# Splitting four gate-unit weights on GpSimd behind the last token-major projection

## The reference

```
p = h @ w_in                                   # (1024 x 1024) @ (1024 x 2500)
sc, q, k, v, iq, ik, iw = split(p)
bg, cg, hv = split(sc, 3)                      # 3 x 512 columns
ya = bg * causal_dwconv(cg * hv, conv_w)       # mixer A: gated short convolution
isc = sum_h relu(iq_h . ik) * iw_h             # mixer B: indexer scores, causal
idx = top_k(isc, 256)                          # 256 keys for each query
yb = softmax(q . k[idx]) @ v[idx]              # 8 heads
x = x + concat(ya, yb) @ w_out
```

## Time and profile before

| | |
|---|---|
| median of 3 runs | 2147.96 us (2147.0 to 2148.61) |
| the profiled execution's own time | 2148.47 us |
| its span | 2146.7 us |
| TensorE busy | 2061.7 us, 96% |
| VectorE, ScalarE, GpSimd busy | 64%, 51%, 52% |
| granted TensorE clock, mean | 0.989 |

### The profile page before, as it was taken

The page is one execution under the profiler, slowest core; times in us unless marked ns, Lnnn a source line. Parts: engine busy times, 40 slices in busy tenths (PEclk is TensorE's granted clock), DMA queues, the critical chain, the costliest instruction groups (busy, mean ns, idle before and its releaser), DMA issues. The chain is left out here.

```text
span 2146.7 us, 30050 instructions
## 1 busy us (share of the span) xinstructions
PE 2061.7 (96%) x11390; PEld 1008.0 (47%) x11390; DVE 1381.4 (64%) x2019; ACT 1092.0 (51%) x1635; POOL 1116.0 (52%) x849
## 2 busy tenths in 40 slices
PE   8989977899999999999999999999999999999998
PEld 5534445644444444444444445664444444444444
DVE  7789988848674674674553045785867377467542
ACT  6468956726664664545332234542656366365520
POOL 6015442243867667657574024414386766856632
PEclk9999999999999999999999999999999999999999
DMA  4001100021112212112231011102121221211212
GB/s 179 19 11 50 35 28 2 14 64 40 51 53 65 59 47 72 55 55 59 69 106 50 0 30 35 45 12 59 40 59 45 74 59 45 74 50 50 59 45 93
DMA packets 186493, 110.20 MB, mean 51 GB/s; under 512 B 4351, under 2 KB 180902, under 8 KB 186358
## 3 DMA queue, kind: packets, MB, share of 16 engines
q1 hardware_dynamic: 185894, 107.00, 16.7%
q0 software_dynamic: 464, 1.39, 0.2%
HBM read 104.18 MB, written 4.19 MB: 50 GB/s over the span
## 5 line engine op out<-in xcount | busy, mean ns | idle before, releaser
L1318 PE MATMUL ps<-arena 128*128 128x512 f16 x2712 | 594.1, 379 | 3.9 <-DVE ps L2952 2.5
L1318 PEld LDWEIGHTS ps<-arena 128*128 128x128 f16 x2712 | 264.8, 98 | 326.6 <-DVE ps L2952 5.5
L1318 PE MATMUL ps<-h_hi,arena 128*128 128x512 f16 x1216 | 372.0, 381 | 4.7 <-DVE arena L3043 4.1
L823 POOL TENSOR_SCALAR w_scaled<-stage 128x1024 f32<-128x1024 f32 (+4 forms) x82 | 82.1, 1002 | 520.2 <-PE ps L1177 348.7
L2961 DVE SCALAR_TENSOR_TENSOR work<-ps,fvec,work 128x1023 f32<-128x1023 f32 (+1 forms) x176 | 221.6, 1279 | 22.1 <-ACT work L2107 19.0
L1318 PE MATMUL ps<-h_lo,arena 128*128 128x512 f16 x608 | 231.7, 381 | 0.0
L1318 PEld LDWEIGHTS ps<-h_hi,arena 128*128 128x128 f16 x1216 | 119.4, 98 | 151.8 <-issue 7.9
L879 POOL TENSOR_TENSOR w_scaled<-stage 128x512 f32<-128x512 f32 (+2 forms) x62 | 70.0, 1129 | 193.6 <-ACT stage L1824 193.4
L1824 ACT ACTIVATE stage<-stage 128x2048 f32<-128x2048 f32 (+2 forms) x62 | 104.5, 1686 | 112.4 <-DMA stage<-in_ffn_w_up_dram 96.1
L829 POOL TENSOR_TENSOR arena<-w_scaled,arena 128x1024 f16<-128x1024 f32 (+4 forms) x82 | 145.0, 1768 | 23.6 <-DVE srch L2723 17.6
L1177 PE MATMUL ps<-h_hi,arena 128*128 128x512 f16 x576 | 150.2, 381 | 2.1 <-ACT small L2006 1.7
(11 more groups left out here) (398 smaller groups left out, 3887.9 us busy)
## 6 DMA issues: line engine op xcount, KB each, us to landing
stage<-in_ffn_w_up_dram SPq DMA_DIRECT2D x84, 512.0 KB, 3.8
stage<-in_ffn_w_down_dram SPq DMA_DIRECT2D x48, 384.0 KB, 3.2
stage<-in_od_w_in_dram SPq DMA_DIRECT2D x20, 512.0 KB, 3.7
stage<-in_ev_w_in_dram SPq DMA_DIRECT2D x12, 512.0 KB, 3.8
arena<-in_x_dram SPq DMA_DIRECT2D x8, 512.0 KB, 5.8
stage<-in_ffn_w_down_dram SPq DMA_DIRECT2D x16, 256.0 KB, 2.7
out_dram<-arena SPq DMA_DIRECT2D x8, 512.0 KB, 3.0
stage<-in_od_w_out_dram SPq DMA_DIRECT2D x12, 256.0 KB, 2.8
```

The lines of the kernel that those rows point to most:

```text
L823: nc.gpsimd.tensor_scalar(scaled, src, W_SCALE, 1.0, ALU.mult, ALU.mult).then_inc(w_parts, 1)
L1318: last = mm(ps[:, bank, :], left, b[:, k, :], start=(fresh and k == 0 and pss == 0), stop=(k == nk - 1 and pss == 2), skip_group_check=True)
```

## The change

Gate units 2 to 5 are no longer put in the ring. GpSimd waits until all eight blocks of the token-major projection are done (`tm_done` 8) and then splits the four one behind another, into `mix_hi` rows 4 to 7 and `mix_lo` rows 0 to 3. No step of the search is waited for by these four. Units 6 and 7 take the ring's slots of units 0 and 1 and wait for these alone; units 8 to 11 wait for unit u - 2 as before. The bits at which the low parts of units 6 to 11 may start are others, and the taps and high parts of mixer A stand at other places among the splits. TensorE's order, VectorE's and ScalarE's programs and all loads are as before.

```diff
-LOW_AT_BIT = {2: 1, 3: 4, 4: 6, 5: 9, 6: 12, 7: 14, 8: 17, 9: 20, 10: 22, 11: 25}
+LOW_AT_BIT = {6: 2, 7: 6, 8: 19, 9: 22, 10: 24, 11: 26}
+AHEAD = range(2, 6)
...
+        def gate_parts(u):
+
+            if u in AHEAD:
+                return mix_hi[:, 4 + u - AHEAD[0], :], mix_lo[:, u - AHEAD[0], :]
+            return w_hi[:, u % 2, :], w_lo[:, u % 2, :]
...
+            def split_gate_unit(u, low_at=None):
+                s, (hi, lo) = u % 2, gate_parts(u)
+                ring = None if u < 6 else ring0["ev_sc"] + (u if u >= 8 else u - 4)
+                split(unit0["ev_sc"] + u, s, stage[:, s, :], w_scaled[:], hi, lo, ring, low_at=low_at)
...
-            for u in range(12):
-                split_ring(unit0["ev_sc"] + u, u, 1024, ring0["ev_sc"] + u if u >= 2 else None, LOW_AT_BIT.get(u))
-                if u >= 3 and u % 3 == 0:
-                    mixer_tap(u // 3 - 1)
-                if u >= 3 and u % 3 == 1:
-                    mixer_high(u // 3 - 1)
+            split_gate_unit(0)
+            split_gate_unit(1)
+            pool.wait_ge(tm_done, NB)
+            for u in AHEAD:
+                split_gate_unit(u)
+            split_gate_unit(6, LOW_AT_BIT[6])
+            mixer_tap(0)
+            split_gate_unit(7, LOW_AT_BIT[7])
+            mixer_high(0)
+            mixer_tap(1)
+            mixer_high(1)
+            split_gate_unit(8, LOW_AT_BIT[8])
+            mixer_tap(2)
+            split_gate_unit(9, LOW_AT_BIT[9])
+            split_gate_unit(10, LOW_AT_BIT[10])
+            mixer_high(2)
+            split_gate_unit(11, LOW_AT_BIT[11])
...
-            def three_pass(slot, nk, hi, lo, k0, out2, first, last_unit, operand_waits={}):
+            def three_pass(slot, nk, hi, lo, k0, out2, first, last_unit, operand_waits={}, parts=None):
+                parts_hi, parts_lo = parts or (w_hi[:, slot, :], w_lo[:, slot, :])
...
-                three_pass(n % 2, 8, h_hi, h_lo, 0, pair(n % 4), True, True).then_inc(unit_done, 1)
+                three_pass(n % 2, 8, h_hi, h_lo, 0, pair(n % 4), True, True, parts=gate_parts(n)).then_inc(unit_done, 1)
```

More of the change, by code:

```diff
@@ L1172, in three_pass @@
                         pe.wait_ge(*operand_waits[k0 + k])
-                    wh = k_of(w_hi[:, slot, :], 8)[:, k, :]
-                    wl = k_of(w_lo[:, slot, :], 8)[:, k, :]
+                    wh, wl = k_of(parts_hi, 8)[:, k, :], k_of(parts_lo, 8)[:, k, :]
                     for pss, (w, a) in enumerate(((wh, hi), (wh, lo), (wl, hi))):
```

## The result

The changed kernel took 2155.11 us (median of 8 runs, 2153.94 to 2158.56), the kernel before 2147.39 us beside it (8 runs, 2145.41 to 2148.61). The ratio is 1.0039, 95% interval 1.0029 to 1.0048: 7.7 us slower. Forecast were 2154.5 us and +6.5 us. The profiled execution of the changed kernel was the slowest of its eight and took 2158.56 us, 10.1 more than the profiled one of before; 1.7 us of that lie ahead of the change. So times in the two traces are counted here from a common mark, the sixteen turns of keys just behind the last projected block.

A forecast was written before the change was run, and what follows sets the result against it. The prediction took the indexer's chain before the gate units, then the search, as the bound. A 12.3 us delay less 5.8 us gained in the search gave +6.5 us, 2154.5 us, range 2145 to 2161.

The forecast's parts named there:

- What bounds: Indexer's VectorE-ScalarE-TensorE chain before 137.5 us, then the search from 148.3 us; lengthening either comes out at the end in full.
- Part 1: Four units split behind the last projection delay VectorE's chain, first gate unit and search by 12.3 us (7.8 to 17.0).
- The 15.1: Alternative delay in us before the gate units, if a port holder blocks the other engine to its own end.
- Part 2: Search with six splits in place of ten: 5.8 us shorter (3 to 12.0), 5.1 of it by bit 19.
- search of about 120 us: Sign that the forecast is right: search length from first to last L2723, 121.5 us before.
- upper bound of 12.0: Most us the search could gain: all the time ScalarE's counts idle for VectorE there.
- Part 3: TensorE's gate units: no wait at unit 8, 3.2 us at unit 9; attention still gains 5.75 us from the search.
- The two meet: At the first early add, TensorE's early unit 0 and VectorE's search both end at 269.6 us, old frame.
- A: Rival: splits fall into VectorE's waits before the gate units, or search gains near 12 us; 2143.2 us, chance 0.17.
- B: Rival: the ends cancel, splits ahead cost 7.8 us and the search gains 7; 2148.8 us, chance 0.16.
- C: Rival: search gains nothing as units 8 and 9 come late, TensorE losing 5.2 and 3.6 us; 2160 to 2161, chance 0.11.
- D: Rival: the four splits begin much later than 113.6 us, through a late `tm_done`; chance 0.01.

The follow-up runs named there:

- the ahead half alone: The kernel before, plus twelve unused GpSimd split instructions behind the last projection, all ten search splits kept: 2160.29 us, ratio 1.0065.
- the repetition: The changed kernel run again unaltered, beside the kernel before: 2155.75 us, ratio 1.0043.
- The best version: The changed kernel, but first ahead unit held to VectorE's first count, most other splits and mixer A's high parts held to bits: 2139.54 us, ratio 0.9964.

## Why the prediction was right, and where it was not

**What bounds.** Right. Two links, the chain in front of the gate units and the search behind; the ahead half alone moved the attention by 12.2 us for 12.3 in front.

**Part 1, +12.3 us.** The mechanism was right: GpSimd busy from 115.5 to 136.4 us (1.7 of that is the later mark), the small instructions mostly at 1.0 to 2.1 us, three L2619 (now L2642) 4.03 for 2.85. The size: 10.50 in the changed kernel, 12.3 with the same forms in the kernel before, and the 1.8 between them lie in the first three sums, where the two engines start within 0.1 us of each other. So 12.3 was within the reach of the method, but no finer. That the first unit and the search start at 149.70 and 160.50, where 149.8 and 160.5 were forecast, is luck: 1.7 us of each lie ahead of the change. The kind that waits was drawn too narrowly: L2615 (now L2638), with one tensor in, took 1.03 us for 0.61. The 15.1 worked out by the rule of the Trainium skill (SBUF — State Buffer, Who interferes with whom) lay above both.

**Part 2, -5.8 us.** This is the term that was mis-sized: the search gained 3.2 us (3.9 in the repetition), 3.7 of it by bit 19, where 5.1 were forecast. (The "search of about 120 us" among the signs does not follow from the forecast itself: 121.5 - 5.8 is 115.7.) Two steps failed. One was to give each collision that goes a gain of about half its length. Bits 10 and 11 together took 4.27 + 2.75 = 7.02 us before and 3.08 + 3.98 = 7.06 in the changed kernel: taken together, bit 10's collision had cost nothing. The other was to ask only which splits leave a bit, with those that stay assumed to meet what they met before. They moved too. A collision is decided by tenths of a microsecond: GpSimd's L830 and L832 start when TensorE gives the slot back or when the tap is done, and TensorE now stood elsewhere against the bits. In the changed kernel's VectorE timeline, at bit 16 (unit 8's pair begins at 222.66 us) and bit 22 (unit 10's pair at 248.19, directly behind unit 9's low part):

```profile
222.99 0.72 DVE L2728 TENSOR_TENSOR srch<-srch 128x2 int32<-128x2 f32 x1
223.75 0.97 DVE L2737 SCALAR_TENSOR_TENSOR srch<-srch 128x2 int32<-128x2 int32 x1
...
249.33 0.99 DVE L2728 TENSOR_TENSOR srch<-srch 128x4 int32<-128x4 f32 x1
250.36 0.97 DVE L2737 SCALAR_TENSOR_TENSOR srch<-srch 128x4 int32<-128x4 int32 x1
```

Each of these is 0.15 or 0.16 us at rest. Bit 16 took 4.12 us in place of the 3.1 forecast; bit 22 took 5.80 for 4.16 before, where no change was forecast; bit 25 took 5.49 for 4.68, where a small gain was, though only 4.17 in the repetition. Bit 13, of which 1.6 was forecast, gave 2.45 (5.85 to 3.40). The kernels with the splits held to a bit show the converse: with as many splits as the change or more, searches of 115.9, 111.0 and 109.9 us. My upper bound of 12.0 from the earlier trace rows was sound: the best searches gained 10.5 and 11.6.

**Part 3.** Unit 9's wait was forecast at 3.2 us and was 3.01. Unit 8's, forecast as none, was 1.88, since bit 19 came 1.4 us later than I had it. Together that is 4.9 us for 3.2, so the good figure for unit 9 alone is luck: the wait at unit 8 had already taken part of it. I counted nothing for the clock behind such a wait: it was 0.56 in the 7 us behind unit 9's in the first trace, some 3 us of work lost (fourteen matmuls in 5.9 us that take 3.0 at full clock), and 1.00 in the repetition. "The two meet" held by luck, with TensorE and VectorE both later than forecast. The 6 us wait ahead of early unit 2 went, and its clock is 1.00, as forecast.

**The sum.** Forecast 12.3 - 5.8 = 6.5. From the mark to the attention, measured 10.5 - 1.5 = 9.0 in one trace and 10.5 - 3.7 = 6.8 in the other; the medians say 7.7. Part 1 was 1.8 us too large, the search's gain 2.6 (5.8 for 3.2). They have opposite signs, so the sum was better than its parts: that it came within 1.2 us of the medians is in part luck.

**The rivals.** A fell with the 10.5. B fell: the cost was above its 7.8. C was partly true: its lateness of units 8 and 9 came (4.9 us of 8.8), but with the search gaining 3.7 by bit 19 TensorE's spare time took most of it, and taking the waits away gave 1.1 us or nothing. D fell.

## What to carry to other kernels

An engine that shares a port has a price by the instruction, not by the microsecond: here a 0.15 us instruction of VectorE with two SBUF operands that met a 1 us GpSimd instruction paid 0.8 us, and a 0.87 us count beside such a one paid nothing. So moving GpSimd work "into a gap" is worth it only where VectorE's instructions of that gap are of the kind that doesn't wait; here the gap was full of the other kind, and holding each instruction at a count, with a wait on a step counter that was there already, gained more (3.7 us, and 7 together with the freed slots) than taking four units out of the search (2.1 us by itself). And when work leaves a stretch, what stays in it moves too: re-time the rest before summing what the leavers give.

## What the runs showed of the hardware

- GpSimd's writing alone costs VectorE's instructions with two SBUF operands nothing: twelve memsets, 0.53 to 0.95 us each, back to back, left instructions of 0.23 us at 0.23.
- Short VectorE instructions with one tensor in wait beside a reading GpSimd as well: a copy of 128x6 took 0.98 us for 0.17 and L2717 1.98 for 0.17 with the splits behind the sums.
- The first meeting differs with the order of the starts: VectorE's first three sums took 3.1 us more than at rest in the kernel where GpSimd was 0.10 us ahead, and 1.2 more where VectorE was 0.03 us ahead.
- Accumulating counts with one SBUF tensor pass beside a busy GpSimd: 640 columns took 0.87 us, as without it, during 5.3 us of back-to-back splits.
- The granted clock doesn't always fall behind the same wait: of two executions of the changed kernel with a wait of 3.0 us at unit 9, one ran the next matmuls at 0.56 of full speed on the mean of 7 us (pairs of 1.01 us: the lower level of 1.2 GHz), the other at 1.00. The twelve units took 2.9 us longer in the first, and the attention came 2.1 us later. The best version shows it at unit 0: behind a wait of 1.69 us, the granted clock from 137 to 142 us was 1.00 in one execution and 0.66 in the other.
